# Summing the left half of some gathered rows on TensorE: five heads of the third token tile

## The chip, the cores and the metric

The kernel runs on one core of a Trainium2 chip. The metric is device time in microseconds (us), the median of the runs shown. A profile of one execution stands beside the times. The engines are called PE (TensorE), DVE (VectorE), ACT (ScalarE), POOL (GpSimd) and SP (SyncE) in the profile. All data are 32-bit floats.

## The reference

The program is two transformer blocks, one after the other. The change lies in the last part of the first block, a layer that picks 16 of 16,384 experts for each token and head, takes a row of a first table (u) for each, and sums rows of a second table (v) weighted by the results:

```python
def chunk(args):
    x_c, i_c, g_c = args
    act = jax.nn.gelu(jnp.einsum('chkd,cd->chk', u_tab[i_c], x_c))
    return jnp.einsum('chk,chkd->cd', g_c * act, v_tab[i_c])
```

There are 512 tokens, 8 heads (h), 16 experts (k) and 1024 columns (d). The second block (sliding-window and latent attention, dilated attention, two cross attentions, two gated feed-forward layers) reads the sum, token by token, so its first half of the tokens can start when their sums are ready.

## The kernel before

**Tiles and units.** The tokens form four tiles t of 128 (a token a partition). The expert layer walks over 32 units (h, t): first the heads of tiles 0 and 1 in turn, then all 8 heads of tile 2, then all 8 of tile 3 (`UNITS`). At each step of the walk two units are worked on: the *dots* of one (row of u times the token, a scalar for each of 16 experts j) and, one unit later, its *combination* (16 rows of v, each times its factor, added up).

**Gathers.** POOL issues an indirect DMA for each row block (`peer_pool`, L2282): 128 rows of 1024 floats, 0.5 MB, into one of 8 slots of a ring, v and u in turn. Before it writes a slot it waits, by `p.claim(("ring", slot), ...)`, for the operation that read the slot's last content. With 8 slots and two tables it runs four experts j ahead.

**The combination.** For tiles 0 and 1, 12 of 16 rows go to PE: ACT makes a 128x128 diagonal matrix of the factors (L2373, four buffers in turn), and PE multiplies it with the row block, two matmuls of 512 columns into two PSUM banks (L2354). DVE adds the other four. For tiles 2 and 3 DVE adds all 16 (L2396 the first, L2398 the others) into `ACC[t]`. Dots are DVE's in all tiles (L2412). At a unit's end ACT applies the gelu (L2380), DVE multiplies by the gates (L2420, signal `factors_ready`).

**What runs beside.** While tiles 2 and 3 are combined, the second block works on the first half of the tokens (`second_pe`, `second_act`, `second_dve`, half 0). Each engine's program interleaves it by hand: after each expert j the call `between` advances the second block by a share of its planned PE cost, 256 shares in all. So the order on an engine is fixed: row j, one share of the second block, row j+1, and so on. The second block's pieces that matter here, by line: products with weights of 256 columns (L2735, `product_pe`) and the down products of the feed-forward layer (L3583) on PE; norm sums (L2805); attention scores (L3043 on PE, read by L3129 and L3133 on DVE), weight transposes (L3052), outputs (L3061) and stores (L3067); silu and product of the feed-forward layer on ACT (L3604) and DVE (L3629); squares and sums for norms (L2778 on ACT, L2785 on DVE), scaled rows (L2848 on DVE). Weights of 1 MB come over SP's queue (L2715) into four wide buffers, each claimed when its last product is done.

**Banks.** Tile sums of tiles 0 and 1 use PSUM banks 0 to 3. The second block's half 0 uses banks 0 and 2 to 7 in its first layer, and bank 1 for the first time in its dilated attention.

## Time and profile before

| | us |
|---|---|
| median of 3 runs | 4095.48 |
| lowest, highest | 4072.05, 4103.37 |
| the profiled execution, time | 4095.35 |
| its span, first to last instruction | 4093.6 |

| stretch of the span, us | what runs |
|---|---|
| 1051 to 1892 | dots of tiles 0 and 1 and the first of tile 2, combination of tiles 0 and 1 |
| 1892 to 2309 | combination of heads 0 to 4 of tile 2, beside the first layer of the second block, half 0 |
| 2309 to 2506 | combination of heads 5 to 7 of tile 2, beside its feed-forward layer |
| 2506 to 3045 | combination of tile 3, beside its second layer |
| 3045 to 4094 | the rest of half 0 and all of half 1 of the second block |

A row of the profile that groups instructions gives line, engine, operation, output and inputs with shapes, count, then busy time in us and the mean duration of one in ns, then the engine's idle time just before them and what ended it. A float matmul appears as two records, so 80 matmuls are 160 records; transposes appear as one.

### The profile page before, as it was taken

Reading aid. Unit: us, or ns where it says so; the run is one execution under the profiler, and the core shown is the slowest. Engines: PE = TensorE matmul, PEld = TensorE weight load, DVE = VectorE, ACT = ScalarE, POOL = GpSimd, SP = SyncE. Lnnn points to the kernel's source line nnn. Section 1 sums busy time; section 2 is a strip of 40 time slices with the busy share of each in tenths; the row PEclk is TensorE's granted clock in tenths of the full one; section 3 lists DMA queues with packets and bytes.
Section 4 is the critical chain, followed back from the end, with each engine's and each line's share of the span. In section 5 each row is a group of like instructions: output and inputs, shape, how many; then the busy total and the mean of one; then the engine's idle time right before and its main releaser. Section 6 shows DMA issues by size and latency. Waiting matters only on the chain. (4 is left out here: it accounts for less than half of the span.)

```text
span 4093.6 us, 40032 instructions
## 1 busy us (share of the span) xinstructions
PE 3448.6 (84%) x14758; PEld 2546.7 (62%) x14758; DVE 2218.7 (54%) x4366; ACT 726.2 (18%) x1627; POOL 1388.2 (34%) x1215
## 2 busy tenths in 40 slices
PE   7889988889867786865777998878998899999999
PEld 3445638778533352523555777667876678887787
DVE  2443044544898878886777668877653420033201
ACT  2121122222221111111222001211012220022200
POOL 0641002220467767666444565545620000000000
PEclk9887798899978898987777999879998999999999
DMA  6230210002799999997767999979972034431343
GB/s 205 72 112 11 70 36 1 1 1 53 264 358 366 362 334 366 369 370 277 269 215 274 391 394 375 324 244 360 390 246 70 32 112 148 151 103 57 108 154 103
DMA packets 449224, 834.05 MB, mean 204 GB/s; under 512 B 46659, under 2 KB 291454, under 8 KB 449022
## 3 DMA queue, kind: packets, MB, share of 16 engines
q0 software_dynamic: 147456, 536.94, 35.3%
q1 hardware_dynamic: 301574, 294.56, 22.5%
q8 instruction: 118, 1.93, 0.2%
q14 instruction: 76, 0.62, 0.0%
HBM read 829.23 MB, written 2.17 MB: 203 GB/s over the span
## 5 line engine op out<-in xcount | busy, mean ns | idle before, releaser
L2735 PE MATMUL banks<-arena 128*128 128x256 f32 (+1 forms) x4992 | 1147.2, 389 | 72.2 <-DMA arena<-in_l_w_up 35.2
L2735 PEld LDWEIGHTS banks<-arena 128*128 128x128 f32 (+1 forms) x4992 | 967.8, 195 | 240.2 <-DMA arena<-in_l_w_up 39.2
L2282 POOL DMA_INDIRECT arena<-in_peer_u,arena x512 | 583.5, 1140 | 495.8 <-DVE arena L2412 183.5
L2282 POOL DMA_INDIRECT arena<-in_peer_v,arena x512 | 583.9, 1140 | 414.9 <-DVE arena L2398 246.2
L2412 DVE CUSTOM_DVE_ANT_0 arena<-arena 128x1024 f32<-128x1024 f32 x512 | 628.1, 1227 | 108.3 <-DMA arena<-in_peer_u,arena 77.1
L2354 PE MATMUL banks<-arena 128*128 128x512 f32 x768 | 412.6, 679 | 212.9 <-ACT arena L2373 79.8
L2354 PEld LDWEIGHTS banks<-arena 128*128 128x128 f32 x768 | 155.8, 215 | 427.3 <-issue 320.0
L2398 DVE SCALAR_TENSOR_TENSOR arena<-arena 128x1024 f32<-128x1024 f32 x316 | 406.2, 1285 | 26.7 <-DMA arena<-in_peer_v,arena 15.6
L3583 PE MATMUL banks<-arena 128*128 128x256 f32 x1408 | 310.5, 378 | 0.0
L3629 DVE TENSOR_TENSOR arena<-banks,arena 128x512 f32<-128x512 f32 x44 | 30.4, 692 | 514.5 <-PE banks L2735 511.5
L3583 PEld LDWEIGHTS banks<-arena 128*128 128x128 f32 x1408 | 265.7, 189 | 38.3
L834 PE MATMUL banks<-arena 128*128 128x512 f32 (+1 forms) x320 | 134.4, 568 | 29.3 <-ACT arena L961 11.5
L3604 ACT ACTIVATE arena<-banks 128x512 f32<-128x512 f32 x44 | 26.3, 598 | 686.1 <-PE banks L2735 656.3
L3043 PE MATMUL banks<-arena 64*128 64x256 f32 (+6 forms) x384 | 130.6, 446 | 2.7 <-issue 1.9
L3090 ACT ACTIVATE arena<-arena 128x256 f32<-128x256 f32 (+3 forms) x128 | 69.4, 542 | 354.9 <-DVE arena L3129 265.1
L547 PE MATMUL banks<-arena 128*128 128x512 f32 (+1 forms) x336 | 131.2, 550 | 0.0
L2067 PE MATMUL banks<-arena 128*128 128x512 f32 (+1 forms) x320 | 121.0, 524 | 3.8 <-ACT arena L1840 3.5
L509 POOL TENSOR_TENSOR arena<-arena 128x2048 f32<-128x2048 f32 x16 | 57.3, 3601 | 196.4 <-ACTq L277 106.7
L3052 PE MATMUL banks<-arena 128*128 128x128 f32 x360 | 78.1, 312 | 53.3 <-ACT arena L3105 25.4
L834 PEld LDWEIGHTS banks<-arena 128*128 128x128 f32 x320 | 63.2, 207 | 94.3 <-issue 81.8
L1565 POOL TENSOR_TENSOR arena<-arena 64x256 f32<-64x256 f32 x24 | 19.1, 794 | 299.9 <-ACT arena L1464 299.0
L3061 PE MATMUL banks<-arena 128*128 128x64 f32 (+1 forms) x720 | 118.5, 299 | 1.2 <-DVE arena L3156 1.1
(338 smaller groups left out, 4270.4 us busy)
## 6 DMA issues: line engine op xcount, KB each, us to landing
arena<-in_l_w_gate SPq DMA_DIRECT2D x44, 1024.0 KB
arena<-in_l_w_up SPq DMA_DIRECT2D x44, 1024.0 KB
arena<-in_l_w_down SPq DMA_DIRECT2D x44, 1024.0 KB
arena<-in_ada_w SPq DMA_DIRECT2D x24, 1024.0 KB, 8.6
arena<-in_l_w_qkv SPq DMA_DIRECT2D x24, 1024.0 KB
arena<-in_w_in SPq DMA_DIRECT2D x33, 512.0 KB
arena<-in_l_w_out SPq DMA_DIRECT2D x16, 1024.0 KB
arena<-in_peer_q_w SPq DMA_DIRECT2D x20, 512.0 KB
```

The source lines that it names most:

```text
L547: ins = p.e.matmul(k.bank[b][0:m, 0:n], k.W[slot][:, c, 0:m], rhs(c), start=c == 0, stop=c == c_n - 1, skip_group_check=True)
L834: ins = p.e.matmul(k.bank[b][0:m, 0:n], k.W[slot][:, c, 0:m], rhs(c), start=c == 0, stop=c == c_n - 1, skip_group_check=True)
L2067: ins = p.e.matmul(k.bank[4][:, cols], ws[j][:, c, :], k.HT[:, c, cols], start=c == 0, stop=c == DC - 1, skip_group_check=True)
L2282: p.e.indirect_dma_start(e.ring[slot], None, tables[table], bass.IndirectOffsetOnAxis(ap=e.IDX[h][:, t, j:j + 1], axis=0)).then_inc(*p.up( ...
L2354: ins = p.e.matmul(k.bank[b], e.diag[x % 4], e.ring[slot][:, half * T:half * T + T], start=h == 0 and j == 0, stop=h == HEADS - 1 and j == ...
L2398: p.e.scalar_tensor_tensor(out=e.ACC[t], in0=e.ring[slot], scalar=factor, in1=e.ACC[t], op0=ALU.mult, op1=ALU.add).then_inc(*p.up(S.rows_a ...
L2412: p.e.tensor_tensor_reduce(out=e.prod, in0=e.ring[slot], in1=e.H2[:, t, :], scale=1.0, scalar=0.0, op0=ALU.mult, op1=ALU.add, accum_out=e. ...
L2735: ins = p.e.matmul(out, left(c), right(c), start=c == 0, stop=c == c_n - 1, skip_group_check=True)
L3043: ins = p.e.matmul(k.bank[b][:, c0:c0 + keys.shape[1]], x.q, keys, start=True, stop=True, skip_group_check=True)
L3052: ins = p.e.transpose(k.bank[4][:, j * P:j * P + P], a.S[u % 2][:, j * P:j * P + P], k.ident)
L3061: ins = p.e.matmul(k.bank[5][:, 0:x.w], a.PT[u % 2][:, j * P:j * P + P], values, start=j == 0, stop=j == len(x.values) - 1, skip_group_che ...
L3583: ins = p.e.matmul(k.bank[4 + o // 2][:, o % 2 * TH:o % 2 * TH + TH], w[:, r, P * o:P * o + P], a.hid[:, (i - 1) % 2, TH * r:TH * r + TH], ...
```

## The change

For units (0..4, 2), the first five heads of the third tile, the row sum is split by columns. DVE adds columns 512 to 1023 only. ACT makes a diagonal of the factors for each of their 80 rows, and PE multiplies it with columns 0 to 511 of the row block, accumulating all 80 in bank 1. After the fifth head DVE waits for the last of these matmuls and copies bank 1 into the left half of `ACC[2]`; heads 5 to 7 are added over the whole width as before. A slot of the ring that holds such a row is written again only after both readers are done.

```diff
+LEFT = 5
+def left_on_pe(unit):
+    return unit is not None and unit[1] == 2 and unit[0] < LEFT
...
 # POOL, before it writes a slot
+        if ("ring left", slot) in p.over:
+            p.wait_ge(*p.over.pop(("ring left", slot)))
...
             p.claim(("ring", slot), S.rows_added, (h, t, j))
+            if left_on_pe((h, t)):
+                p.claim(("ring left", slot), S.rows_combined, (h, t, j))
...
 # PE, before the share of the second block that belongs to j
+            if left_on_pe(combine):
+                h, t = combine
+                slot = slot_of["v", h, t, j]
+                if h == 0 and j == 0:
+                    p.claim(("bank", 1), S.tile_added, (t, "left"))
+                p.wait_ge(S.diagonal_ready, (h, t, j))
+                p.wait_ge(S.landed(f"row{slot}"), ("v", h, t, j))
+                p.e.matmul(k.bank[1], e.diag[x % 4], e.ring[slot][:, 0:T], start=h == 0 and j == 0, stop=h == LEFT - 1 and j == KN - 1,
+                           skip_group_check=True).then_inc(*p.up(S.rows_combined, (h, t, j)))
+                x += 1
...
 # ACT
-            if combine and j in on_pe(combine[1]):
+            if combine and (j in on_pe(combine[1]) or left_on_pe(combine)):
...
 # DVE
+                cols = slice(T if left_on_pe(combine) else 0, D)
+                acc, row = e.ACC[t][:, cols], e.ring[slot][:, cols]
...
+        if combine == (LEFT - 1, 2):
+            p.wait_ge(S.rows_combined, (*combine, KN - 1))
+            p.in_order()
+            p.e.tensor_copy(e.ACC[2][:, 0:T], k.bank[1]).then_inc(*p.up(S.tile_added, (2, "left")))
```

The order on PE, in the products that follow the attention of head 2. Lines moved with the edit: L2735, L2805 and L3067 of before are L2765, L2835 and L3097 of the changed kernel, and L2377 is the new matmul. A row with "x8" is eight matmuls in a row. Before:

```order
L3067 MATMUL banks<-arena 128x128
L2735 MATMUL banks<-arena 128x256 x64
L2805 MATMUL banks<-arena 128x256 x4
L2735 MATMUL banks<-arena 128x256 x32
L3043 MATMUL banks<-arena 128x256 x2
```

The same place in the changed kernel:

```order
L3097 MATMUL banks<-arena 128x128
L2765 MATMUL banks<-arena 128x256 x4
L2377 MATMUL banks<-arena 128x512
L2765 MATMUL banks<-arena 128x256 x8
L2377 MATMUL banks<-arena 128x512
L2765 MATMUL banks<-arena 128x256 x8
L2377 MATMUL banks<-arena 128x512
L2765 MATMUL banks<-arena 128x256 x8
L2377 MATMUL banks<-arena 128x512
```

What was one uninterrupted run of 64 products now has a matmul of 512 columns behind every eighth product.

The order on PE in the attention. L3043, L3052, L3061, L3067 of before are L3073, L3082, L3091, L3097 of the changed kernel:

```order
L3091 MATMUL banks<-arena 128x64 x2
L2377 MATMUL banks<-arena 128x512
L3073 MATMUL banks<-arena 128x128
L3082 MATMUL banks<-arena 128x128
L3091 MATMUL banks<-arena 128x64 x2
L3073 MATMUL banks<-arena 128x256
L3097 MATMUL banks<-arena 128x128
```

Here the new matmul stands behind the outputs of one attention unit and ahead of the scores (L3073) of the next.

The order on DVE at the end of the fifth head. L2398, L2412, L2420 and L3629 of before are L2422, L2438, L2446 and L3659 of the changed kernel. Before:

```order
L2398 SCALAR_TENSOR_TENSOR arena<-arena 128x1024
L2412 ISA arena<-arena 128x1024
L2412 ISA arena 128x1
L2420 TENSOR_TENSOR arena<-arena 128x16
L2398 SCALAR_TENSOR_TENSOR arena<-arena 128x1024
```

In the changed kernel:

```order
L2422 SCALAR_TENSOR_TENSOR arena<-arena 128x512
L2438 ISA arena<-arena 128x1024
L2438 ISA arena 128x1
L2446 TENSOR_TENSOR arena<-arena 128x16
L2451 COPY arena<-banks 128x512
L2422 SCALAR_TENSOR_TENSOR arena<-arena 128x1024
```

The add of a row is half as wide up to here, and the copy out of PSUM stands between the factors and the first full-width add.

## Rows read from the trace of the kernel before

**Rows 1.** Busy time by stretch: window, then each engine's busy us (instructions), PE's clock, DMA.
```profile
core 0: us, PE busy (x) PEld busy (x) DVE busy (x) ACT busy (x) POOL busy (x), PEclk, DMA share, GB/s
1892.00:2246.00 354.00, 259.11 (x997) 196.96 (x998) 270.64 (x511) 74.74 (x191) 148.44 (x131) 0.75 0.71 243
2246.00:2309.00 63.00, 55.29 (x241) 46.82 (x240) 42.38 (x53) 4.58 (x6) 35.90 (x34) 0.95 1.03 396
```

**Rows 2.** Who waited for whom, 1892 to 2246: total us, times, longest.
```profile
POOL arena L2282 <- DVE arena L2398: 95.6, 29, 9.7
...
DVE arena L3145 <- PE banks L3052: 19.7, 17, 3.0
...
PE banks L2805 <- DVE arena L2785: 12.0, 1, 12.0
```

**Rows 3.** The chain of waits by line, shares of 2640 to 2801 (tile 3, second layer).
```profile
by line: PE banks L2735 39.9%; issue 6.2%; DVE arena L2398 5.6%; PE banks L3061 4.5%; PE banks L3052 4.2%; DVE arena L2412 3.8%; DVE arena L3156 2.4%; DVE arena L2844 2.2%; PE banks L3043 2.0%; DVE arena L2793 1.7%; DVE arena L3133 1.3%; PE
```

**Rows 4.** Groups by line, with shapes: full-width add; half-width add elsewhere; diagonal on ACT.
```profile
L2398 DVE SCALAR_TENSOR_TENSOR arena<-arena 128x1024 f32<-128x1024 f32 x64 | 82.3, 1286 | 2.6 <-DMA arena<-in_peer_v,arena 0.4
...
L2656 DVE SCALAR_TENSOR_TENSOR arena<-arena 128x512 f32<-128x512 f32 x6 | 4.2, 692 | 0.2
...
L2373 ACT ACTIVATE arena<-arena 128x128 f32<-128x128 f32 x48 | 17.0, 395 | 43.9 <-PE banks L2354 38.7 <-issue 4.7 <-DVE arena L2420 0.5
```

**Rows 5.** PE, order of time and chain (start us, us, records); windows as rows 1.
```profile
1726.56 5.43 PE L2354 MATMUL banks<-arena 128*128 128x512 f32 x12 [0.85 <-issue]
...
1197.24 3.78 PE L2354 MATMUL banks<-arena 128*128 128x512 f32 x4 [12.18 <-issue]
...
2952.66 13.86 PE banks L2735 x64
...
1727.00:1731.00 4.00, 4.00 (x11) 1.74 (x10) 3.79 (x11) 2.91 (x7) 2.90 (x4) 1.00 1.04 390
1197.00:1201.00 4.00, 3.76 (x5) 1.59 (x6) 3.83 (x10) 1.25 (x4) 0.00 (x0) 0.50 0.93 374
```

**Rows 6.** Busy time by stretch, columns as in rows 1: three product runs.
```profile
1930.00:1950.00 20.00, 20.00 (x96) 17.51 (x95) 18.68 (x24) 1.20 (x2) 14.01 (x13) 1.00 0.78 282
2122.00:2150.00 28.00, 28.00 (x124) 24.29 (x125) 23.92 (x30) 1.90 (x3) 20.46 (x17) 0.95 0.88 312
2164.00:2175.00 11.00, 11.00 (x52) 9.62 (x51) 10.22 (x13) 1.02 (x3) 8.67 (x8) 1.00 0.71 229
```

**Rows 7.** The same: three attention stretches, and their sum.
```profile
1982.00:2085.00 103.00, 71.31 (x249) 47.44 (x248) 74.53 (x197) 29.54 (x95) 31.25 (x30) 0.70 0.56 186
2085.00:2122.00 37.00, 26.08 (x95) 17.74 (x95) 28.53 (x73) 9.73 (x31) 12.56 (x12) 0.64 0.69 224
2175.00:2212.00 37.00, 22.34 (x80) 16.13 (x80) 23.39 (x48) 8.41 (x26) 10.74 (x11) 0.60 0.60 202
sum 177.00, PE 119.73 PEld 81.31 DVE 126.46 ACT 47.68 POOL 54.55; mean PE 39.91 PEld 27.10 DVE 42.15 ACT 15.89 POOL 18.18
```

**Rows 8.** PE and DVE in order of time around one attention unit.
```profile
2108.97 0.74 PE L3043 MATMUL banks<-arena 96*128 96x128 f32 x2
...
2109.60 1.29 DVE L2398 SCALAR_TENSOR_TENSOR arena<-arena 128x1024 f32<-128x1024 f32 x1
2110.92 0.29 DVE L3129 CUSTOM_DVE_ANT_0 arena<-banks,arena 128x128 f32<-128x128 f32 x1
```

**Rows 9.** PE in order of time, 1894 to 1930: norms at the start.
```profile
1919.22 3.78 PE L2805 MATMUL banks<-arena 128*128 128x256 f32 x8 [11.99 <-DVE arena L2785]
1927.24 3.19 PE L2735 MATMUL banks<-arena 128*128 128x256 f32 x7 [4.24 <-DVE arena L2848]
```

**Rows 10.** Groups by line, 2246 to 2309 (head 4, beside the feed-forward layer).
```profile
L2735 PE MATMUL banks<-arena 128*128 128x256 f32 x177 | 42.5, 400 | 7.7 <-DMA arena<-in_l_w_up 4.0 <-DMA arena<-in_l_w_gate 3.7
```

**Rows 11.** ACT and DVE in order of time at two unit ends.
```profile
2165.24 0.22 ACT L2380 ACTIVATE arena<-arena 128x16 f32<-128x16 f32 x1 [8.55 <-DVE arena L2412]
...
2308.67 0.18 DVE L2420 TENSOR_TENSOR arena<-arena 128x16 f32<-128x16 f32 x1 [8.46 <-ACT arena L2380]
```

More of the change, by code:

```diff
@@ L2394, in peer_dve @@
                 p.wait_ge(S.landed(f"row{slot}"), ("v", h, t, j))
+                cols = slice(T if left_on_pe(combine) else 0, D)
+                acc, row = e.ACC[t][:, cols], e.ring[slot][:, cols]
                 if h == 0 and j == (3 if t < 2 else 0):
-                    p.e.tensor_scalar(e.ACC[t], e.ring[slot], factor, None, ALU.mult).then_inc(*p.up(S.rows_added, (h, t, j)))
+                    p.e.tensor_scalar(acc, row, factor, None, ALU.mult).then_inc(*p.up(S.rows_added, (h, t, j)))
                 else:
-                    p.e.scalar_tensor_tensor(out=e.ACC[t], in0=e.ring[slot], scalar=factor, in1=e.ACC[t], op0=ALU.mult,
+                    p.e.scalar_tensor_tensor(out=acc, in0=row, scalar=factor, in1=acc, op0=ALU.mult,
                                              op1=ALU.add).then_inc(*p.up(S.rows_added, (h, t, j)))
@@ L2409, in peer_dve @@
                         p.wait_ge(S.diagonal_ready, (*was, on_pe(was[1])[-1]))
+                    elif left_on_pe(was):
+                        p.wait_ge(S.diagonal_ready, (*was, KN - 1))
                 p.in_order()
```

## The prediction, made before the changed kernel ran

> **What bounds the kernel now.** The busy times by stretch come first. From 1892 to 2246, beside heads 0 to 3 of tile 2, no engine is full: VectorE is busy 270.6 of 354 us (76%), TensorE's matmuls 259.1 (73%), and the granted clock is 0.75, so TensorE stands at its lower level, 1.2 GHz, for half of the time [rows 1]. From 2246 to 2309, beside head 4, TensorE is busy 55.3 of 63 us and the DMA share is 1.03 with 396 GB/s [rows 1]. The average over the first stretch hides two kinds of time, which the windows separate. In runs of products TensorE is busy every microsecond (20.00 of 20, 28.00 of 28, 11.00 of 11) at a clock of 0.95 to 1.00 while VectorE has a few per cent to spare [rows 6]. In the attention of the second block both engines have holes: over three stretches of 177 us together TensorE is busy 119.7 and VectorE 126.5, at clocks of 0.60 to 0.70 [rows 7].
>
> The list of waits says what the adds of rows hold up. Their direct waiter is the gather queue (95.6 us), which refills a slot behind an add [rows 2]; that costs nothing as long as VectorE never starves for rows. VectorE's own largest wait is for TensorE's transposes, 19.7 us [rows 2]. The chain of waits reaches back into the same kind of work beside tile 3, 2640 to 2801: products of L2735 hold 39.9% of it, adds of rows (L2398) 5.6% [rows 3]. That is 9.0 of 161 us, so 7 adds of 1.285 us, of the 32 of the two units there. Only about a fifth of the adds lie on the path, and a product run is on it whole. The change takes from the first kind and adds to the second.
>
> **VectorE's side.** An add of 1024 columns takes 1286 ns, one of 512 columns, elsewhere in the program, 692 ns [rows 4]. 80 of them (5 heads, 16 experts; the first, a plain multiply, is cheaper) save 80 x 0.594 = 47.5 us of busy time. At a fifth on the path that is about 10 us.
>
> **TensorE's side.** A float matmul is two records. 64 records of 256 columns take 13.86 us on the chain at the full clock, 0.217 us each, so one of 512 columns 0.433 and the new matmul 0.87 us. The nearest rows agree: 12 records of 512 columns take 5.43 us where the clock is full, 0.45 each with the tail; 4 take 3.78 us where it is 0.50, so 1.89 us a matmul at the lower level [rows 5]. 80 matmuls are 69 us at the full clock, more than VectorE gives up. What counts is where they stand. Read from the order on TensorE, the 80 fall into four kinds:
>
> - *33 in product runs outside the feed-forward layer*: behind every eighth product (11 in unit (0, 2), 3 in (1, 2), 8 in (2, 2), 11 in (3, 2)). TensorE has no hole there [rows 6], a step of eight products takes 16 x 0.217 = 3.46 us and VectorE is busy 93, 85 and 93% of it, so VectorE's saved time is not seen and TensorE's is paid: 33 x 0.87 = 28.7 us. Bounds: nothing is hidden where TensorE never idles, so not below 27; all at the lower level, 57.
> - *8 around norms*: TensorE waits there anyway, 11.99 us for VectorE's L2785 in one case [rows 9]. The matmuls go into the holes: 0 us. Without that cover they cost 7.
> - *23 in the attention*. The new matmul stands between the outputs of one attention unit and the scores of the next, while VectorE does the add of the same expert. In the row shown, scores end at 2109.71, and their reader L3129 starts at 2110.92, directly behind the add that began at 2109.60 [rows 8]. So the scores had 1.2 us to spare. Now they come 0.87 to 1.89 us later, and the reader could start 0.59 us earlier. Per site that is between -0.59 (the scores are still in time) and +0.7 us (1.89 against a slack of 1.2), if this slack is typical. Bounds for 23: -14 and +16. The signs nearly cancel; I take -5, since the work in the holes also raises the granted clock in part of these 177 us.
> - *16 beside head 4*: 13.9 us. TensorE waits 7.7 us for weights there [rows 10], which the new work can fill, if the weights come no later. That leaves 6.2, at most 13.9; I take 7, near the lower end, because the transfers are at their limit [rows 1] and go on while TensorE computes.
>
> **ACT's side.** 80 diagonals of 395 ns [rows 4] are 32 us on an engine that is busy 74.7 of 354 us [rows 1]. A diagonal waits for ACT's earlier work. At a unit's start it comes behind the gelu (2165.24 + 0.22 us), the gates and its own 0.4, so near 2166.2 [rows 11], while TensorE is in a product run from 2164 on [rows 6]: up to 2 us late. Most others stand behind ACT work that is long done, since ACT is idle four fifths of the time. I take 2 us in all, at most 5 x 2 for the five unit starts and as much again within units, 20 us.
>
> **Slots.** The gather of a slot now also waits for TensorE. Queued behind a held gather are all later ones on POOL, so VectorE's next dots and adds wait for them. The ring holds four experts, 4 x 3.46 = 13.8 us of a product run, and both engines work through the same order, so TensorE must fall far behind VectorE before it holds a gather. Beside head 4 it may: there VectorE waits at the end 8.46 us for ACT, which waits for TensorE [rows 11], so it was ahead by that much. A held gather falls into this wait, and so do the new wait for the last matmul and the copy (0.69 us, as the 692 ns row) at the end of head 4, ahead of the first full-width add. I take 0; if this cover is gone, it is 8.5 us.
>
> **Sum**, against the profiled execution's 4095.35 us (the runs' median is 4095.48): 28.7 + 0 - 5 + 7 + 2 + 0 = 33, so 4128 us. Nothing later absorbs it: the stretch up to 3045 is one fixed order, and half 1 starts when it ends.
>
> **Rivals.**
>
> *Relief of the busiest engine (faster).* VectorE is the busiest engine of the stretch. If all 64 adds before 2246 were on the path, 38 us would go, and with TensorE's additions all in holes the time were 4057. For it speaks only the average; against it the product runs, where TensorE has no hole [rows 6]. The Trainium skill, Perfetto Trace Analysis, "Identifying the Most-Contended Engine", would choose this: it takes occupancy for VectorE and LDWEIGHTS time for TensorE, and says to improve the engine with the highest share first. By its measure VectorE has 76% and TensorE 197.0 of 354, 56%. No row here shows that the rule decides at this place.
>
> *The clock (no loss).* In the attention stretches VectorE idles 177 - 126.5 = 50.5 us, waiting for others. If TensorE went to 2.4 GHz there, at most half of this, 25 us, would go, and with the shorter adds (23 x 0.59 = 14) the attention gives 39 us, which just pays for 38: 4095. It is decided by whether the granted clock of these stretches rises from 0.60 to 0.70 to nearly 1. For it speaks that after TensorE was busy without a hole the clock is full [rows 6]; against it, that the units' own waits for ACT and VectorE stay. I give it partial weight: between 4095 and 4112. The Trainium skill, TensorE: Matmul & The Clock Gate, "Why this matters for your kernels", says to keep TensorE busy to hold the full clock; the rows agree in direction.
>
> *TensorE's new work is on the path nearly everywhere (slower).* The attention takes +16, head 4 takes 13.9, diagonals 5, the held gathers 5: 28.7 + 16 + 13.9 + 5 + 5 = 69, so 4164 us. It decides if the clock stays low in the attention, so that a matmul there costs 1.89 us where 1.2 are free.
>
> **How the numbers follow.** The forecast (4112 to 4141) has 0.5. The clock rival (4085 to 4112) 0.16; relief (under 4085) 0.06, of which half under 4054; the slower rival (4141 to 4185) 0.28. The range 4090 to 4165 leaves out a tenth below and a tenth above. One per cent, about what a measurement can tell here from no change (the three runs spread over 0.8%), is 41 us: faster than 4054.5: 0.03; slower than 4136.4: the slower rival and part of the forecast's upper end, 0.35; between them 0.62.
>
> **What would show it.** In the changed profile: the added matmuls beside L2735 at about 0.87 us a pair and a product run of eight plus one at 4.3 us a step; TensorE's busy time up by some 70 us; the adds at about 0.69 us; the first stretch (units up to head 3) longer by 20 to 30 us, head 4 by 5 to 10; from 2506's counterpart on the same durations as before. The forecast is wrong if the attention stretches change by over 15 us either way, if the product runs do not stretch, or if gathers held by TensorE starve VectorE in or behind head 4.

## The result, and the profile after

The changed kernel takes 4117.7 us, the median of 16 runs (4094.6 to 4158.1). The kernel before takes 4071.3 us beside it, also over 16 runs (4058.9 to 4103.4). The ratio is 1.0104 with a 95% interval of 1.0084 to 1.0123, so the change costs 42 us (34 to 50). The ratio and its interval leave out two slow executions, the profiled one of 4158.1 us here and one of 6961.4 us in the second set below, and where the two profiles of the changed kernel differ the second is the one to go by. The ratio is the recorded one and not the quotient of the two medians, which is 1.0114; a cost in us is the ratio's share of the median of before. The change is slower by about one per cent; the interval reaches to both sides of the one per cent that the prediction names.

The forecast was 4128 us, and 4117.7 lies in its range. The kernel before is itself 24 us lower here than the execution of 4095.4 us on which the sum stood, so it is the ratio that says what the change costs: 42 us, where the sum had 33, just below the interval.

The profiled execution of the changed kernel took 4158.1 us. A second profile of the same kernel has a span of 4091.6 us, 64.7 less. Of these, 36.0 us lie ahead of the changed units (head 0's unit starts at 1896.1 and 1860.1 us) and 25.5 behind the last add of the layer (1075.8 and 1050.3 us; 1050.2 before), where the code is the same. So only the stretches are compared below, in both profiles, each from its own start.

The page of the changed kernel, first profile:

```profile
span 4156.3 us, 40599 instructions
...
PE 3542.1 (85%) x14918; PEld 2591.9 (62%) x14918; DVE 2174.0 (52%) x4367; ACT 750.7 (18%) x1707; POOL 1382.1 (33%) x1215
```

DVE's busy time is 44.7 us below the 2218.7 of before. PE has 160 more records, 80 matmuls of two.

Busy time by stretch of the same profile, columns as in [rows 1], which it answers (beside heads 0 to 3, then beside head 4):

```profile
1896.00:2281.00 385.00, 304.24 (x1117) 207.05 (x1118) 237.03 (x512) 94.09 (x257) 143.20 (x132) 0.83 0.66 223
2281.00:2351.00 70.00, 69.42 (x290) 54.34 (x289) 33.98 (x53) 9.46 (x22) 37.20 (x34) 1.00 1.02 372
```

The first stretch has grown from 354 to 385 us although DVE has 34 us less to do in it. PE has 45 us more, at a higher granted clock (0.83 against 0.75). Beside head 4 PE has no hole left: 69.42 of 70 us, at the full clock.

Groups of instructions by line with shapes, first profile, both stretches (count, busy us, mean ns of one, idle time before):

```profile
L2377 PE MATMUL banks<-arena 128*128 128x512 f32 x160 | 95.9, 687 | 15.3 <-ACT arena L2395 14.8 <-issue 0.5
...
L2422 DVE SCALAR_TENSOR_TENSOR arena<-arena 128x512 f32<-128x512 f32 x79 | 59.5, 753 | 6.0 <-DMA arena<-in_peer_v,arena 3.1
L2395 ACT ACTIVATE arena<-arena 128x128 f32<-128x128 f32 x80 | 28.8, 391 | 10.3 <-PE banks L2377 9.0 <-DVE arena L2446 1.4
```

Three things stand here. A half-width add takes 753 ns, not the 692 of the nearest row [rows 4]. The diagonals cost what they were priced at, 391 ns. And PE waited 14.8 us for them (L2377 behind ACT's L2395), where the sum had 2.

**Where the time went.** The adds of rows (VectorE's, one for each row) stand in the same order in every version, so their start times give a ledger. The table shows how much later, against the profile of before and counted from the start of head 0's unit, each piece of the stretch adds; "rows" are the rows moved in a piece.

| piece | rows | change, 1st profile | change, 2nd |
|---|---|---|---|
| to row 3 of head 1 | 14 in products, 5 at norms | +6.2 | +6.0 |
| to row 6 of head 2 | 19 in attention | +14.3 | +7.4 |
| to row 4 of head 3 | 12 in products, 2 at norms | +11.9 | +12.3 |
| to row 8 of head 3 | 4 in attention | +0.3 | +0.3 |
| to row 1 of head 4 | 7 in products, 1 at a norm, row 0 of head 4 | +0.8 | +0.8 |
| to row 1 of head 5 | 15 beside head 4 | +0.6 | +0.7 |
| sum | | +34.1 | +27.5 |

Of the first piece 3 us have to be added. The profile of before holds a small disturbance near its 60th us that 11 of the 14 profiles taken here do not have, those of the changed kernel among them (last section); the same code without it is 3 us shorter at row 3 of head 1 (the experiment on head 4 alone, whose first four heads are unchanged, shows -2.9). So by the two profiles the change costs 37 and 31 us up to row 1 of head 5, beside the 42 (34 to 50) of the timed runs above and the 28 (12 to 44) of a second set of them. The two profiles, of one and the same kernel, differ by 6.9 us in the first attention piece: a difference of that size between single profiles is not yet an effect.

### The profile page after: what moved, and what is told of

Its sections match the earlier page's. It is cut to its first block and busy times, and to the rows that moved or that the text cites. A ratio compares the mean times of both kernels' runs of the same rounds, so it can differ in the third digit from the quotient of the medians.

```text
span 4156.3 us, 40599 instructions
## 1 busy us (share of the span) xinstructions
PE 3542.1 (85%) x14918; PEld 2591.9 (62%) x14918; DVE 2174.0 (52%) x4367; ACT 750.7 (18%) x1707; POOL 1382.1 (33%) x1215
## 3 DMA queue, kind: packets, MB, share of 16 engines
q1 hardware_dynamic: 301574, 294.56, 22.1%
## 5 line engine op out<-in xcount | busy, mean ns | idle before, releaser
L2765 PE MATMUL banks<-arena 128*128 128x256 f32 (+1 forms) x4992 | 1147.3, 388 | 48.4 <-DVE arena L2878 17.9
L2765 PEld LDWEIGHTS banks<-arena 128*128 128x128 f32 (+1 forms) x4992 | 962.4, 194 | 233.4 <-issue 53.6
L2438 DVE CUSTOM_DVE_ANT_0 arena<-arena 128x1024 f32<-128x1024 f32 x512 | 628.3, 1227 | 113.1 <-DMA arena<-in_peer_u,arena 87.5
L2366 PEld LDWEIGHTS banks<-arena 128*128 128x128 f32 x768 | 156.6, 216 | 416.9 <-issue 310.3
L2422 DVE SCALAR_TENSOR_TENSOR arena<-arena 128x1024 f32<-128x1024 f32 (+1 forms) x316 | 364.2, 1152 | 30.4 <-DMA arena<-in_peer_v,arena 18.5
L3659 DVE TENSOR_TENSOR arena<-banks,arena 128x512 f32<-128x512 f32 x44 | 30.4, 692 | 513.9 <-PE banks L2765 513.6
L3613 PEld LDWEIGHTS banks<-arena 128*128 128x128 f32 x1408 | 265.7, 189 | 40.0 <-issue 1.9
L3073 PE MATMUL banks<-arena 64*128 64x256 f32 (+6 forms) x384 | 132.9, 455 | 2.8 <-issue 2.1
L3091 PE MATMUL banks<-arena 128*128 128x64 f32 (+1 forms) x720 | 123.2, 309 | 1.2 <-DVE arena L3186 1.1
L3082 PE MATMUL banks<-arena 128*128 128x128 f32 x360 | 80.3, 321 | 50.2 <-ACT arena L3135 22.6
L3091 PEld LDWEIGHTS banks<-arena 128*128 128x128 f32 x720 | 118.1, 236 | 5.3 <-issue 3.9
L834 PEld LDWEIGHTS banks<-arena 128*128 128x128 f32 x320 | 62.5, 205 | 91.8 <-issue 80.0
```

Source lines behind the costliest of these rows:

```text
L834: ins = p.e.matmul(k.bank[b][0:m, 0:n], k.W[slot][:, c, 0:m], rhs(c), start=c == 0, stop=c == c_n - 1, skip_group_check=True)
L2366: ins = p.e.matmul(k.bank[b], e.diag[x % 4], e.ring[slot][:, half * T:half * T + T], start=h == 0 and j == 0, stop=h == HEADS - 1 and j == ...
L2422: p.e.scalar_tensor_tensor(out=acc, in0=row, scalar=factor, in1=acc, op0=ALU.mult, op1=ALU.add).then_inc(*p.up(S.rows_added, (h, t, j)))
L2438: p.e.tensor_tensor_reduce(out=e.prod, in0=e.ring[slot], in1=e.H2[:, t, :], scale=1.0, scalar=0.0, op0=ALU.mult, op1=ALU.add, accum_out=e. ...
L2765: ins = p.e.matmul(out, left(c), right(c), start=c == 0, stop=c == c_n - 1, skip_group_check=True)
L3073: ins = p.e.matmul(k.bank[b][:, c0:c0 + keys.shape[1]], x.q, keys, start=True, stop=True, skip_group_check=True)
```

## The experiments

"Stretch" is the time of the five units of heads 0 to 4, from the start of head 0's unit. It is 416.8 us in the profile of before, 413.8 without the disturbance, 454.6 and 447.9 with the change. Pieces are those of the table above. A stretch comes from one profile. The ratios come from timed runs beside which the kernel before took 4071.0 us (the two halves, the constant operands, the changed kernel again), 4080.0 (diagonals one ahead, attention rows, product rows, the clock) and 4065.2 (head 4, the better place).

### The two halves of the change apart

First VectorE's part alone; the left half of the 80 rows is then added nowhere. The copy out of bank 1 stays.

```diff
 # PE: the block "if left_on_pe(combine)" is left out, as are its diagonals on ACT,
 # the claim on the slot and the wait for the last matmul
 # DVE, as in the changed kernel
                 cols = slice(T if left_on_pe(combine) else 0, D)
```

> VectorE's part of the change alone: the adds of heads 0 to 4 of tile 2 are 512 columns wide, TensorE and ACT do nothing new, the slots wait for VectorE alone (the left half of the sum is left out). My prediction: a fifth of 47 us is on the path, so 8 to 12 us faster than before, most of it in units (1, 2) to (3, 2). Rival 'relief of the busiest engine': about 38 us faster. Rival 'VectorE's time was never on the path': 0 to 3 us.

Measured: 4052.2 us, ratio 0.994 (0.9911 to 0.9969), so 24 us faster (13 to 36). The stretch takes 401.2 us, 12.6 less than the undisturbed 413.8. Of the 42.6 us that the shorter adds save (80 x (1.286 - 0.753)) the profile gives back three tenths. The busy times of its first stretch, columns as in [rows 1]:

```profile
1863.50:2200.00 336.50, 246.92 (x979) 187.96 (x980) 234.37 (x507) 72.51 (x188) 144.62 (x127) 0.77 0.73 251
```

DVE is now busy 234.4 of 336.5 us, 70% instead of 76%. The attention of heads 1 and 2 (19 rows) has 8.3 us of the gain, the rest is spread. In this version VectorE waits 19.4 us for gathered rows in the five units, more than half of it beside head 4, where it waited 3.5 before. What that takes from the gain was not tried.

Then TensorE's and ACT's part alone, with the adds as wide as before:

```diff
-                cols = slice(T if left_on_pe(combine) else 0, D)
+                cols = slice(0, D)
...
-            p.e.tensor_copy(e.ACC[2][:, 0:T], k.bank[1]).then_inc(...)
+            p.e.tensor_copy(e.prod[:, 0:T], k.bank[1]).then_inc(...)
```

> TensorE's and ACT's part alone: diagonals, matmuls, waits and the shared slots as in the change, but VectorE adds all 1024 columns as before, and the copy goes to a spare buffer. My prediction: the loss of the change plus what e1 gains, so 50 to 55 us slower than before if the two parts add up; the attention gives +10 or more here, since the reader of the scores can't start earlier. If the parts do not add up (the narrower add is worth something only where the matmul does not stand in front of the scores), the loss equals that of the change, about 42 us.

Measured: 4112.3 us, ratio 1.0119 (1.0054 to 1.0184), stretch 460.7, which is 46.9 over the undisturbed one. The two halves add up: 46.9 - 12.6 = 34.3, and the change as a whole has 34.1 in the second profile and 40.8 in the first. TensorE's part costs more than three times what VectorE's gives back in the same profiles.

Then the same matmuls in the same places, but with constant operands, so that they wait for no diagonal and no row and hold no slot. Their product is not the left half of the sum:

```diff
-                p.wait_ge(S.diagonal_ready, (h, t, j))
-                p.wait_ge(S.landed(f"row{slot}"), ("v", h, t, j))
-                p.e.matmul(k.bank[1], e.diag[x % 4], e.ring[slot][:, 0:T], ...)
+                p.wait_ge(S.sines_ready, (1, 1))
+                p.e.matmul(k.bank[1], k.ident, k.cos64, ...)
```

> The change with the 80 matmuls on constant data: no diagonal on ACT, no wait for a diagonal or a landing, no claim on the slots; size and place as in the change, VectorE's adds half as wide (the left half of the sum is wrong). If TensorE's array time is the cost, this is as slow as the change, 1.010 of before. If waits for diagonals, rows or held gathers are a good part (the surprise is unit (1, 2), 127.5 us against 109.7), it is 10 to 20 us faster than the change, mostly in that unit.

Measured: 4094.9 us, ratio 1.0057 (1.0029 to 1.0085), stretch 435.6. That is 12.3 and 19.0 us less than in the two profiles of the change. The attention of heads 1 and 2 costs 1.4 us in it instead of 7.4 and 14.3, the piece behind it with 12 rows in products 11.1 instead of 11.9 and 12.3. So in the attention it is mostly the waits of the matmuls that cost, in the products the matmuls themselves. This version takes away three things at once, the diagonals, the waits for rows and the claims on slots; the next experiment takes the diagonals alone.

The changed kernel once more, timed beside these versions:

> The changed kernel once more, for a second profile: the units (1, 2) and (2, 2) are longer by about 18 and 11 us again if that is the change and not the one execution; the time after the last gather (1121 us in the first profile against 1103 before) comes back near 1103.

Measured: 4106.8 us, ratio 1.0069 (1.003 to 1.0108); its stretch of 447.9 is in the table above.

### The diagonals

ACT makes the diagonal of row j + 1 while row j is in work, so the matmul of j never waits for the ACT work of its own turn:

```diff
-            if combine and (j in on_pe(combine[1]) or left_on_pe(combine)):
+            if left_on_pe(combine):
+                todo = [0, 1] if j == 0 else [j + 1] if j + 1 < KN else []
+            else:
+                todo = [j] if combine and j in on_pe(combine[1]) else []
+            for d in todo:
```

> The change with each diagonal made one expert earlier on ACT (row j+1's at expert j), so that it stands ahead of that share's attention work. The matmuls on constant data (435.6 us from 1892 to 2309's counterpart, the change 447.9 and 454.6) say that waits of the new matmul cost 12 to 19 us. Theory 'late diagonals': 8 to 15 us of it come back here, and nearly all in the attention. Theory 'rows and slots': the stretch stays at 445 to 455.

Measured: 4104.4 us, ratio 1.006 (1.0025 to 1.0095), stretch 440.2. By the profiles that is 7.7 and 14.4 us below the change; the timed ratios alone would not separate them. It is mostly the attention that gets cheaper: 3.1 us instead of 7.4 and 14.3. The 4.6 us between this stretch and the 435.6 with constant operands may be waits for rows, for slots and for the diagonals that are still late; they were not taken apart. The list of waits shows what the diagonals did. PE in the changed kernel (second profile), then in this one (us in total, times, longest):

```profile
PE banks L2377 <- ACT arena L2395: 15.1, 13, 4.5
```

```profile
PE banks L2377 <- ACT arena L2399: 7.5, 3, 4.2
```

13 waits became 3. The two longest that stay, PE in order of time, stand right behind the starts of the units of heads 0 and 2 (at 1866.0 and 2065.9), where no earlier diagonal can be made:

```profile
1866.70 2.04 PE L2377 MATMUL banks<-arena 128*128 128x512 f32 x2 [4.16 <-ACT arena L2399]
...
2066.59 1.21 PE L2377 MATMUL banks<-arena 128*128 128x512 f32 x2 [2.19 <-ACT arena L2399]
```

How such a wait delays the attention stands in the changed kernel's second profile in order of time:

```profile
2034.48 0.52 PE L3091 MATMUL banks<-arena 128*128 128x64 f32 x2
...
2035.83 0.39 ACT L2395 ACTIVATE arena<-arena 128x128 f32<-128x128 f32 x1
2036.27 0.50 PEld L2377 LDWEIGHTS banks<-arena 128*128 128x128 f32 x2 [1.46 <-ACT arena L2395]
2036.27 2.08 PE L2377 MATMUL banks<-arena 128*128 128x512 f32 x2 [1.27 <-ACT arena L2395]
...
2038.14 0.64 PE L3073 MATMUL banks<-arena 96*128 96x128 f32 x2
...
2038.95 0.29 DVE L3159 CUSTOM_DVE_ANT_0 arena<-banks,arena 128x128 f32<-128x128 f32 x1 [2.74 <-PE banks L3073]
```

PE is done with the outputs (L3091) at 2035.0 and waits 1.27 us for the diagonal. The new matmul then takes 2.08 us, and only then come the scores (L3073). DVE, which needs them for the next step, stands for 2.74 us. At the site shown in [rows 8] the scores had 1.2 us to spare; the diagonal alone uses that up.

### The kinds of rows apart

The rows that go to TensorE were made a list, so that each kind can be moved alone. The rows of the right kind only are split; the copy at the end becomes an add, since the left half of `ACC[2]` is then in use.

```diff
+ROWS = [...]    # (head, expert)
+def left_on_pe(unit, j):
+    return unit is not None and unit[1] == 2 and (unit[0], j) in ROWS
...
-            p.e.tensor_copy(e.ACC[2][:, 0:T], k.bank[1])
+            p.e.tensor_tensor(e.ACC[2][:, 0:T], k.bank[1], e.ACC[2][:, 0:T], ALU.add)
```

The 23 rows in the attention: (1, 3..15), (2, 0..5), (3, 4..7).

> Only the 23 rows whose matmul stands in the attention go to TensorE; the other 57 are added full width by VectorE; bank 1 is added to the sum at the end of head 3. If the attention alone explains the loss (my prediction had put it at -5): stretch longer by 12 to 18 us against 416.8. If the signs cancel there as predicted: 412 to 420.

Measured: 4077.5 us, ratio 0.9999 (0.9977 to 1.002), stretch 426.7. This profile has the disturbance of before, so it is compared with 416.8: +9.9. At the end of the attention (row 8 of head 3) it is 15.1 us late, at row 1 of head 5 12.4. The timed runs show no loss: their interval, from 9 us of gain to 8 of loss, holds none of these figures. So how the attention loses time is seen in profiles, and how much it costs in the whole kernel stays open.

The 33 rows in product runs: (0, 5..15), (1, 0..2), (2, 6..13), (3, 0..3), (3, 8..11), (3, 13..15).

> Only the 33 rows whose matmul stands in product runs outside the feed-forward layer go to TensorE, nothing in the attention or beside head 4. My prediction: 33 x 0.87 = 28.7 us longer. The steps of the change's profile suggest less, about 20 (some runs end in a wait that takes up the lag): 434 to 440 for the stretch against 416.8.

Measured: 4093.0 us, ratio 1.0057 (1.0025 to 1.0089), so 23 us slower (10 to 36). The stretch takes 432.1, 18.3 over the undisturbed one. At row 1 of head 4 it is 23.6 us late, 26.6 against the undisturbed code: 0.81 us for each of the 33 rows. 5.6 us of that go again beside head 4, where PE's 7.7 us of waiting for weights [rows 10] are gone. The group of products by line, PE, that unit:

```profile
L2766 PE MATMUL banks<-arena 128*128 128x256 f32 x184 | 40.4, 379 | 0.3 <-issue 0.3
```

The 16 rows beside head 4, (4, 0..15):

> Only the 16 rows of head 4 go to TensorE, beside the feed-forward layer, where the DMA share is 1.03. My prediction: 6.2 to 13.9 us, taken as 7. The change's steps say: 8 us later in the middle of head 4, all but 1 to 2 us of it gone at the first row of head 5, where the kernel before waits for weights. So 3 to 8 us for head 4 and -6 to 0 for the next unit, 0 to 2 us in both together.

Measured: 4067.8 us, ratio 1.0008 (0.9979 to 1.0038). At row 8 of head 3, where all is still as in before, this version stands 3.1 us earlier (the missing disturbance), at row 11 of head 4 5.2 us later, and at row 1 of head 5 1.5 us earlier: net 1.6 us for 16 rows. The groups by line, PE, head 4's unit in this kernel, then the unit behind it (head 5) in before and in the changed kernel (second profile):

```profile
L2766 PE MATMUL banks<-arena 128*128 128x256 f32 x194 | 44.1, 378 | 0.0
```

```profile
L2735 PE MATMUL banks<-arena 128*128 128x256 f32 x170 | 39.3, 391 | 2.2 <-DMA arena<-in_l_w_up 2.2
```

```profile
L2765 PE MATMUL banks<-arena 128*128 128x256 f32 x159 | 35.2, 379 | 0.9 <-DMA arena<-in_l_w_gate 0.9
```

The 7.7 us for which PE waited for weights in head 4 [rows 10] are 0.0: the weights come while the new matmuls run. In the next unit that wait shrinks too, from 2.2 to 0.9 us in the changed kernel, and this unit takes 56.1 us instead of 59.3. So part of what head 4 loses is made good one unit later.

In the timed runs the three kinds have 0 us (9 of gain to 8 of loss), 23 (10 to 36) and 3 (9 of gain to 15 of loss). Only the loss of the product rows is clear of zero there; the split between the other two rests on the profiles.

### The clock alone

The kernel before, with three matmuls of 128 columns on constants ahead of each transpose of weights and each output in the attention of half 0, results unused. They keep TensorE occupied and do nothing else; VectorE's work is as before. They also stand in the attention beside tile 3, so the timed runs hold more of them than the stretch does.

```diff
-    if a.h_id == 0:
+    if a.h_id == 0 and b not in (4, 5):
         return
...
+    n += 2 * (a.h_id == 0)
     for _ in range(n):
         p.e.matmul(k.bank[b][:, 0:P], k.ident, k.ident, start=True, stop=True, skip_group_check=True)
```

> The kernel before with three 128x128 dummy matmuls ahead of each weight transpose and each output of the attention of half 0, where TensorE mostly waits; nothing of the row sums is changed. If more TensorE work in the holes lifts the granted clock of the attention (0.60 to 0.71 before) and shortens its work, the stretch 1892 to 2309 gets 5 to 20 us shorter and the clock there is 0.8 or more. If the clock is not worth anything there, or the dummies stand in the way, it is unchanged or longer by up to 10 us at any clock.

Measured: 4129.4 us, ratio 1.0119 (1.0073 to 1.0165), stretch 441.5, 24.7 over before, which has the same disturbance. Busy time by stretch for the units of heads 1 and 2, columns as in [rows 1], before:

```profile
1975.50:2085.30 109.80, 78.11 (x280) 52.88 (x280) 81.02 (x207) 30.55 (x98) 36.53 (x34) 0.71 0.59 196
2085.30:2165.50 80.20, 63.48 (x254) 49.52 (x252) 63.63 (x119) 15.24 (x38) 36.31 (x31) 0.80 0.77 266
```

and the same two units with the extra matmuls, then the group of these matmuls over the stretch:

```profile
1940.50:2060.80 120.30, 90.13 (x464) 69.61 (x463) 80.87 (x206) 30.31 (x98) 38.18 (x34) 0.84 0.54 181
2060.80:2143.90 83.10, 68.51 (x371) 56.85 (x370) 63.64 (x118) 15.10 (x38) 36.08 (x31) 0.96 0.74 258
```

```profile
L2707 PE MATMUL banks<-arena 128*128 128x128 f32 x402 | 69.1, 319 | 27.2 <-ACT arena L3106 15.0 <-DVE arena L3163 10.4 <-ACT arena L3103 0.7
```

The granted clock rises from 0.71 to 0.84 and from 0.80 to 0.96, DVE's busy time stays (81.02 and 80.87, 63.63 and 63.64), and the units take 10.5 and 2.9 us longer. Head 3's unit loses the most, 12.8 us (92.8 against 80.0), at a granted clock of 0.87 against 0.77: VectorE's wait for the outputs, ahead of which extra matmuls stand (in before L3156 waits for L3061), grows there from 7.6 to 18.7 us. The extra matmuls are busy for 69.1 us, and the stretch grows by 24.7, so two thirds of them are hidden or made good; the rise of the clock does not pay for the rest. What a higher clock would be worth without the matmuls' own time this experiment does not say.

### A better place in the attention

The 23 attention rows, with the diagonals one ahead:

```diff
+            todo = [d for d in (j, j + 1) if d < KN and left_on_pe(combine, d) and d not in made]
```

> The 23 attention rows alone, their diagonals one expert earlier. The same rows with diagonals in their old place made the stretch 1892 to 2309 longer by 10 us (426.7 against 416.8) and the later steps by 13. If late diagonals were the cost there, 6 to 12 of this is gone: 415 to 421 for the stretch. If the matmul itself, ahead of the scores, is the cost, 424 or more.

Measured: 4060.0 us, ratio 1.0003 (0.998 to 1.0025), stretch 412.9, against the undisturbed 413.8. From row 3 of head 1 to row 8 of head 3, the whole of these rows, the shift grows by 3.7 us; with late diagonals it was 15.1.

Then also with the matmul moved behind the scores of the next attention unit, where DVE has its next input already:

```diff
-                p.e.matmul(k.bank[1], e.diag[x % 4], ...)
+                k.pending = h, t, j, slot, x % 4
...
 # PE, right behind the scores of an attention unit, or at the end of the share of j
+            left_matmul(k, p)
```

> As the run before it, and each of the 23 matmuls stands behind the next scores that TensorE issues, no longer in front of them, so VectorE can read the scores while TensorE sums the row. If what is left of the cost is the place, the gain of VectorE's shorter adds (8 us in the attention when they stood alone) shows: 408 to 415 for the stretch, a little faster than the kernel before. If the matmul costs wherever it stands, since TensorE's next piece comes late instead, no better than the run before.

Measured: 4068.0 us, ratio 0.9996 (0.9968 to 1.0024), stretch 405.4, 8.4 below the undisturbed. Over the attention the rows now gain 4.3 us instead of costing 3.7. DVE's wait for scores, before, in the changed kernel (second profile), with the 23 rows only, with the diagonals ahead, and behind the scores, five lists of waits:

```profile
DVE arena L3129 <- PE banks L3043: 3.6, 8, 0.7
```

```profile
DVE arena L3159 <- PE banks L3073: 18.1, 10, 5.0
```

```profile
DVE arena L3160 <- PE banks L3074: 14.3, 12, 2.7
```

```profile
DVE arena L3165 <- PE banks L3079: 11.7, 12, 2.5
```

```profile
DVE arena L3192 <- PE banks L3099: 19.7, 16, 3.0
...
DVE arena L3176 <- PE banks L3089: 2.2, 4, 0.8
```

The wait for scores was 3.6 us before the change, went to 18.1, and is 2.2 us with the matmul behind them. A second reader of the scores (L3133 before) goes the same way: 0.5 us, 11.4 in the changed kernel, 1.4 here. The wait for the transposes (first line of the last fence) is 19.7 us, exactly what it was before [rows 2]. The matmul now stands where neither is held up. The timed ratios of the three placements, 0.9999, 1.0003 and 0.9996, do not separate them.

The last version, meant to beat both kernels, is the above with seven rows around norms added, (0, 1..4), (2, 14), (2, 15) and (3, 12), and no row in a product run.

```diff
+ROWS = [(0, 1..4), (1, 3..15), (2, 0..5), (2, 14), (2, 15), (3, 4..7), (3, 12)]
```

> The version that the runs point to: the 23 attention rows and 7 of the 8 rows at norms (the first excepted) on TensorE, diagonals one expert ahead, matmuls behind the scores, nothing in product runs or beside head 4. The norm rows cost nothing in the change's profile (shift of 0.1 us after them): 405 to 415 for the stretch, a ratio of 0.997 to 0.999 if the theory holds; 1.000 to 1.003 if the matmul costs in every place.

Measured: 4058.1 us, ratio 1.0007 (0.9976 to 1.0038), stretch 403.4. The profile has 10 us less than the undisturbed stretch, but the timed runs show no gain, and leave 10 us of gain and 15 of loss open. The ratio lies where it was expected if the matmul cost in every place, and the interval holds the other case too, so the timed runs do not decide between them. It beats the changed kernel, not the kernel before.

## Why the prediction was right

The direction and the range were right: TensorE's new work costs more than VectorE's relief gives, and the product runs are where most of it is paid. That the total came so near is partly luck. By the second profile and the 3 us of the disturbance, up to row 1 of head 5:

| term | forecast, us | measured, us |
|---|---|---|
| products, with the norms | 28.7 | 22.1 |
| attention and diagonals | -5 + 2 | +7.7 |
| head 4 | +7 | +0.7 |
| sum | 33 | 30.5 |

Three terms were off, by 6.6 and 6.3 us too high and by 10.7 too low, and these nearly cancel. The absolute time of 4128 stood on an execution 24 us above the median of 16, so its nearness to 4117.7 says little by itself.

**Product runs (33 rows): predicted 28.7, bounds 27 to 57. Right in mechanism; the size came out below the lower bound.** PE in order of time, second profile, in the run of the order shown ahead of the prediction:

```profile
2108.90 3.75 PE L2765 MATMUL banks<-arena 128*128 128x256 f32 x16
2112.48 1.02 PE L2377 MATMUL banks<-arena 128*128 128x512 f32 x2
2113.34 3.63 PE L2765 MATMUL banks<-arena 128*128 128x256 f32 x16
2116.81 1.02 PE L2377 MATMUL banks<-arena 128*128 128x512 f32 x2
2117.66 3.63 PE L2765 MATMUL banks<-arena 128*128 128x256 f32 x16
2121.13 1.02 PE L2377 MATMUL banks<-arena 128*128 128x512 f32 x2
```

A step takes 2117.66 - 2113.34 = 4.32 us, forecast 4.3. The window of the run at the start, where [rows 6] has 18.68 us of DVE, has less DVE and as full a PE:

```profile
1897.00:1917.00 20.00, 20.00 (x83) 15.20 (x83) 15.28 (x24) 2.64 (x7) 13.38 (x10) 1.00 0.79 278
```

The three product pieces together cost 21.9 and 22.1 us in the changed kernel (with the 3 us of the disturbance) and 26.6 alone. The lower bound of 27 came from holding that a run without holes hides nothing. Locally that is so. Ledger and steps part at the runs' ends, above all in head 3's last run, where 7 rows cost 4.7 us alone and 0.8 in the changed kernel. What takes up the 4 us was not isolated. The upper bound of 57 prices a matmul at the lower level at twice 0.87 us; at the 1.89 of its own row it is 62. Neither was reached.

**Attention (23 rows): predicted -5, bounds -14 and +16, and late diagonals +2, at most 20.** Measured together: +7.7 in the second profile (+14.6 in the first), and +15.1 alone, of which 9.9 are left at the stretch's end. In the profiles this step has the wrong sign, though it stays within its bounds. It took the gain of the shorter add and the loss of the later scores as nearly equal, from one site where the scores had 1.2 us to spare, "if this slack is typical". It is not: of the 32 reads by L3129 in the profile of before, 8 had to wait for their scores (the list above), so they had nothing to spare, and the others started 0.1 to 2.9 us behind them. Both parts of the loss were too small. The diagonals stand behind ACT's own attention work, 13 waits of 15.1 us in total; "ACT is idle four fifths of the time" says nothing of the moment at which one is wanted. Making them one ahead took 7.7 and 14.4 us off the change, and 11.4 off the 23 rows. The rest is the matmul itself, ahead of the scores: moved behind them it gives another 8.0 us (from +3.7 to -4.3). The -5 of the sum is what this other placement has. The timed runs of the 23 rows alone, 9 us of gain to 8 of loss, hold the forecast of -5: it is the profiles that go against it, not the timed runs.

**Head 4 (16 rows): predicted +7, between 6.2 and 13.9. Measured: +1.6 alone, about 0.7 in the change.** The lower bound was too high since it counted only the wait for weights in the unit itself as cover; against the undisturbed code row 11 of head 4 is 8.3 us late and row 1 of head 5 only 1.6, so the rest is made good around the change of units.

**Norms (8 rows): 0, and the final copy and the slots: 0. Right.** Row 3 of head 0, behind the first rows at norms, stands 0.1 us from its place in before; the norm rows further on were not moved alone. The gather queue waited for TensorE as it was foreseen that it might, 116.5 us in 40 waits in the first profile, and no loss of VectorE by it shows. The longest waits of the first stretch there (us in total, times, longest):

```profile
POOL arena L2294 <- PE banks L2377: 116.5, 40, 11.1
```

VectorE did starve for rows more than before. In the group L2422 above the half-width adds waited 3.1 us for rows of v, and the dots, from the same list, waited 8.0 us for rows of u:

```profile
L2438 DVE CUSTOM_DVE_ANT_0 arena<-arena 128x1024 f32<-128x1024 f32 x81 | 99.3, 1226 | 11.1 <-DMA arena<-in_peer_u,arena 8.0
```

Over the same five units these waits were 1.9 and 1.6 us before. But the version with constant operands, which holds no slot for TensorE, has 3.4 and 8.3, VectorE's part alone has 19.4 us together, and TensorE's part alone, which does hold the slots, has 1.2. The clock experiment, with adds as wide as before and no shared slots, has 10.6 together. So the waits for rows are not TensorE holding slots; what they cost, and what brings them, was not taken apart.

**VectorE's gain: predicted 10 us in the whole path.** Alone it is 12.6 us in the profile, 24 (13 to 36) in the timed runs, of 42.6 saved. A fifth was too low; it was three tenths in the profile and a little over half in the timed runs, whose interval is wide (13 to 36 of 42.6).

**The rivals.** *Relief of the busiest engine* fell with the first two experiments: all of VectorE's part gives 12.6 to 24 us, not 38, and TensorE's part costs 46.9, not nothing. The Trainium skill, Perfetto Trace Analysis, "Identifying the Most-Contended Engine", would have the engine with the highest share improved first; VectorE was that at 76%, and by relieving it alone the time did fall, by 24 us. What the runs go against is to take the relief for the whole effect: the work went to an engine that is full in the product runs, and the change as a whole lost 42 us. *The clock* fell with the ledger: it needed the attention to give 39 us, and the attention cost 7.7 and 14.6 while the granted clock of the first stretch rose from 0.75 to 0.83. Its own experiment shows the clock rise (0.71 to 0.84, 0.80 to 0.96) and no net gain, but since the extra matmuls are on the path it does not say what the clock alone is worth. The Trainium skill, TensorE: Matmul & The Clock Gate, "Why this matters for your kernels", advises to keep TensorE busy for the clock; the rows agree that busy work raised the granted clock, and show that raising it with work on the path lost 24.7 us in the stretch. *New work on the path nearly everywhere* had the attention nearer (+16 against 7.7 and 14.6), the diagonals not far off (5), and head 4 and the held gathers wrong (13.9 and 5 against 1.6 and 0).

**Signs that were named ahead.** Steps of 4.3 us: seen. Adds at 0.69: 0.753. PE busier by 70 us: by 93.5 in the first profile and 17.3 in the second, whose mean granted clocks are 0.896 and 0.917 (0.900 before), so the busy time of the whole program is no measure of 80 matmuls; in the two stretches of the first profile it is 59 us, 373.7 against 314.4. First stretch longer by 20 to 30, head 4 by 5 to 10: +31 and +7 (+24 and +7 in the second profile), of which the next unit gave back 3 (59.3 to 56.2). The same durations further on: the first seven units of the tile behind take 485.0 before and 489.0 and 488.2 after, so they nearly are. Of the three signs of being wrong none is there, one only just: the attention moved by 7.7 us, and by 14.6 in the first profile, where 15 was named; the product runs stretched; VectorE was not starved by held gathers.

## What to carry to other kernels

Before moving work from a busy engine to a less busy one, read whether the second is idle at the places where the work would stand: a matmul in a run without holes is paid for the most part (0.7 to 0.8 us of 0.87 here); beside waits for transfers, in head 4, a matmul cost about 0.1 us; the first at the norms cost nothing that the ledger shows. In a chain that goes back and forth between engines, the place within the step decides more than the amount: in the profiles the same 23 matmuls cost 15 us ahead of the scores with operands just made, 4 with operands made one step early, and gained 4 behind the scores. The timed runs do not separate the three, so this is a reading of single profiles that agree with the lists of waits. An engine with four fifths of its time free can still be late; a short operation that another engine waits for is put one step ahead of its use.

## What the runs showed of the hardware

The half-width add takes 753 ns where the same form at another line took 692 [rows 4]; both run over 128x512 floats. The first reads a slot of the ring and a strided half of the accumulator; which of it costs the 61 ns was not tried.

The kernel before does not always run its own code alike. PE in order of time near the 60th us of the stretch, in the profile of before:

```profile
1949.53 2.29 PE L3239 MATMUL banks<-arena 128*128 128x128 f32 x17
1952.30 0.47 PE L3239 MATMUL banks<-arena 128*128 128x128 f32 x2 [0.48 <-issue]
1953.02 0.36 PE L3239 MATMUL banks<-arena 128*128 128x128 f32 x1 [0.25 <-issue]
...
1955.16 2.39 PE L3239 MATMUL banks<-arena 128*128 128x128 f32 x10 [0.33 <-issue]
1957.35 3.62 PE L3178 MATMUL banks<-arena 128*128 128x512 f32 x4
```

Amid a run of matmuls PE stands still five times for 0.25 to 0.48 us with nothing to wait for that the profile shows, and then runs at its lower level: 4 records of 128x512 take 3.62 us, where they take 1.88 in the changed kernel. Up to row 12 of head 0 that costs 5 us, of which 3 stay. Gaps of this kind are there in the profiles of before, of the 23 attention rows (two of 0.9 us) and of the clock experiment, and in none of the other eleven; one profile each says nothing on what brings them. Without such a gap the same unchanged code still differs by some 2 us at row 3 of head 1.

Outside the stretch the differences are larger. Head 0's unit starts between 1857.6 and 1866.2 us in ten of the profiles and between 1882.0 and 1898.5 in four (before, the changed kernel's first, the constant operands, the attention rows), behind the same code. The time behind the layer's last add is 1050.2 to 1052.7 us in eleven, and 1075.8 and 1070.9 in the changed kernel's first and with constant operands. So the two steps are of 16 to 41 us and of 18 to 26 us, and the 16 timed runs of the kernel before spread over 44; what brings the steps was not tried. A difference between two whole times should not be read as an effect of an edit before the stretch that was edited has been compared, and one of 3 to 5 us not before such a gap has been ruled out.
